# Rewriting how sums are opened and when VectorE makes its keys in a two-block transformer on one core

## The reference

```
kk = (k * k_k).reshape(b, s, h, n)
kk = kk / jnp.maximum(jnp.linalg.norm(kk, axis=-1, keepdims=True), 1e-12)
k = k * (1.0 + (a - 1.0) * k_a)
b_h = kk * a_h
def step(state, inp):
    r_t, w_t, k_t, v_t, kk_t, b_t = inp
    sa = jnp.einsum('bhvk,bhk->bhv', state, -kk_t)
    state = (state * w_t[:, :, None, :] + sa[..., None] * b_t[:, :, None, :]
             + v_t[..., None] * k_t[:, :, None, :])
    return state, jnp.einsum('bhvk,bhk->bhv', state, r_t)
_, y = lax.scan(step, state0, xs)
y = ((y - mu) * lax.rsqrt(var + RW_GN_EPS)).reshape(b, s, c) * lnx_g + lnx_b
y = (y + bonus.reshape(b, s, c)) * g
```

## Time and profile before

| what | value |
|---|---|
| median of 3 runs | 3160.74 us (3159.27 to 3164.67) |
| the profiled execution, time | 3164.66 us |
| its span in the trace | 3162.6 us |
| TensorE busy | 3033.9 us, 96% of the span |
| VectorE, ScalarE, GpSimd busy | 799.9, 469.8, 106.6 us |
| chain that ended last | TensorE 79%, SyncE's queue 10%, DMA 4%, VectorE 3% |
| mean granted TensorE clock | 0.981 |

### The profile page before, as it was taken

The page is one execution under the profiler, slowest core; times in us unless marked ns, Lnnn a source line. Parts: engine busy times, 40 slices in busy tenths (PEclk is TensorE's granted clock), DMA queues, the critical chain, the costliest instruction groups (busy, mean ns, idle before and its releaser), DMA issues.

```text
span 3162.6 us, 39204 instructions
## 1 busy us (share of the span) xinstructions
PE 3033.9 (96%) x16547; PEld 2126.2 (67%) x16547; DVE 799.9 (25%) x1677; ACT 469.8 (15%) x1074; POOL 106.6 (3%) x118
## 2 busy tenths in 40 slices
PE   7999998999999999999998999998899999999998
PEld 3566666577777777677786577786666666666665
DVE  2566666410020044300255400034000001001001
ACT  2332332000010022200121200122000000000001
POOL 1121121000000000000000000000000000000000
PEclk8999999999999999999998999998999999999999
DMA  7333117454444433254401244441999999999996
GB/s 249 115 113 127 47 55 275 152 184 151 142 145 159 133 133 100 68 158 143 154 36 41 91 158 147 151 121 37 380 384 382 384 381 382 382 383 382 380 383 255
DMA packets 403488, 636.07 MB, mean 201 GB/s; under 512 B 11247, under 2 KB 276054, under 8 KB 396030
## 3 DMA queue, kind: packets, MB, share of 16 engines
q1 hardware_dynamic: 397981, 612.29, 55.7%
q0 software_dynamic: 5344, 21.46, 1.9%
HBM read 632.51 MB, written 1.20 MB: 200 GB/s over the span
## 4 chain that ended last, share of the span: by engine, by line
PE 79%; SPq 10%; DMA 4%; DVE 3%; issue 1%; ACT 1%; DVEq 1%; PEld 0%; PEldq 0%; ACTq 0%
PE PS L925 18%; PE PS L933 7%; PE PS L1394 7%; PE PS L3835 5%; SPq L852 5%; PE PS L3862 4%; SPq L3713 3%; PE PS L3887 3%; PE PS L3850 3%; PE PS L701 2%; PE PS L1970 2%; PE PS L991 2%; PE PS L3290 2%; PE PS L1966 2%; PE PS L675 1%; PE PS L1544 1%
## 5 line engine op out<-in xcount | busy, mean ns | idle before, releaser
L925 PE MATMUL PS<-XT,WO 128*128 128x256 f32 x1344 | 296.2, 379 | 0.1
L925 PE MATMUL PS<-XT,WF 128*128 128x256 f32 x1344 | 294.6, 379 | 0.0
L925 PEld LDWEIGHTS PS<-XT,WO 128*128 128x128 f32 x1344 | 255.2, 190 | 50.5 <-issue 17.7
L925 PEld LDWEIGHTS PS<-XT,WF 128*128 128x128 f32 x1344 | 255.3, 190 | 46.2 <-issue 12.9
L1394 PE MATMUL PS<-XT,WH 128*128 128x512 f32 x512 | 241.6, 597 | 1.8 <-ACT XT L476 1.8
L952 DVE TENSOR_TENSOR scratch<-scratch,PS 128x256 f32<-128x256 f32 x70 | 29.5, 421 | 660.5 <-ACT scratch L942 660.2
L4122 DVE TENSOR_TENSOR scratch<-scratch,PS 128x128 f32<-128x128 f32 x84 | 24.2, 288 | 557.0 <-ACT scratch L4020 557.0
L3835 PEld LDWEIGHTS PS<-scratch,WO 128*128 128x128 f32 x1344 | 155.3, 192 | 12.6 <-issue 12.0
L3835 PEld LDWEIGHTS PS<-scratch,WF 128*128 128x128 f32 x1344 | 155.2, 192 | 12.4 <-issue 11.0
L3835 PE MATMUL PS<-scratch,WF 128*128 128x128 f32 x1344 | 157.0, 275 | 1.2 <-ACT scratch L3999 1.2
L3835 PE MATMUL PS<-scratch,WO 128*128 128x128 f32 x1344 | 157.0, 275 | 0.4 <-DMA WO<-in_moe_wu 0.4
(11 more groups left out here) (579 smaller groups left out, 4060.4 us busy)
## 6 DMA issues: line engine op xcount, KB each, us to landing
XT<-in_moe_wg SPq DMA_DIRECT2D x70, 1024.0 KB, 11.1
scratch<-in_moe_wu SPq DMA_DIRECT2D x70, 1024.0 KB, 13.3
WO<-in_ada_w SPq DMA_DIRECT2D x36, 1024.0 KB, 7.2
OT<-in_moe_wd SPq DMA_DIRECT2D x36, 1024.0 KB, 13.9
WF<-in_moe_wg SPq DMA_DIRECT2D x21, 1024.0 KB, 14.3
WF<-in_moe_wu SPq DMA_DIRECT2D x21, 1024.0 KB, 17.0
WF<-in_moe_wd SPq DMA_DIRECT2D x21, 1024.0 KB, 14.3
WO<-in_moe_wg SPq DMA_DIRECT2D x21, 1024.0 KB, 14.5
```

The lines of the kernel that those rows point to most:

```text
L925: mm = nc.tensor.matmul(k.PS[:, 4 + f, w * n:(w + 1) * n], slot.gu[:, w, kb, f * P:(f + 1) * P], rhs(kb), start=kb == 0, stop=kb == KB - 1)
```

## The change

There are four edits. Sums are no longer opened by `zero_sum` in the dense nets, the DeltaNet heads and the scan; their first product has `start=True` instead. `rw_tilde_vector` is split into `rw_keys_scaled_vector` (three operations) and `rw_decayed_vector` (three and the signal `til`), and for round 1 they run inside round 0's scan, behind z and behind the negated rn. "tkv" moves from place 0 to place 1 of level 2. At level 4 of round 1, `rw_out_vector` comes ahead of `mla_rope_vector`.

```diff
-def turn_tensor(k, pe, slots, order, rnds, rhs, n, hid, acc):
+def turn_tensor(k, pe, slots, order, rnds, rhs, n, hid, acc, opens=None):
...
-                                      slot.dn[:, f, half * 512:(half + 1) * 512], start=False, stop=False)
+                                      slot.dn[:, f, half * 512:(half + 1) * 512], start=(what, s, f) == opens, stop=False)
...
-    zero_sum(k, True, range(4))
-    turn_tensor(k, pe, slots, TURN[2:8], first, rhs, L, k.hid, range(4))
+    turn_tensor(k, pe, slots, TURN[2:8], first, rhs, L, k.hid, range(4), ("down", 0, 0))
...
-            zero_sum(k, True, (4,))
             project(24, 27)
...
             mm = nc.tensor.matmul(ps[:, 4, c], k.vn[:, d, :], k.att[h % 2][:, d, tile, :],
-                                  start=False, stop=t == 3 and d == 1)
+                                  start=t == 0 and d == 0, stop=t == 3 and d == 1, skip_group_check=True)
...
-    elif step == (2, 0):
+    elif step == (2, 1):
         rw_tokens_tensor(k, pe, rnd, "tkv")
-    elif step == (2, 1):
         rw_tokens_tensor(k, pe, rnd, "tk")
...
     rw_u_tensor(k, pe, rnd, 0)
-    zero_sum(k, True, (4, 5))
     for j, hh in heads:
-        nc.tensor.matmul(z(j, hh), k.tok[:, 2, 2 * j, ROWS[hh]], k.tok[:, 0, 2 * j, ROWS[hh]], start=False, stop=False)
+        nc.tensor.matmul(z(j, hh), k.tok[:, 2, 2 * j, ROWS[hh]], k.tok[:, 0, 2 * j, ROWS[hh]], start=j == 0, stop=False,
+                         skip_group_check=True)
...
-    zero_sum(k, True, (2, 3))
     for j, hh in heads:
         nc.tensor.matmul(rn(j, hh), k.gr[0][:, hh, 2 * j + 1, :], k.tok[:, 0, 2 * j + 1, ROWS[hh]],
-                         start=False, stop=False)
+                         start=j == 0, stop=False, skip_group_check=True)
...
-def rw_tilde_vector(k, dve, rnd):
+def rw_keys_scaled_vector(k, dve, rnd):
...
     tt(k.kk, k.kk, k.rtm, ALU.mult)
     dve.drain()
     tt(bt, k.kk, k.ra[:, 2 * rnd:2 * rnd + 2, :], ALU.mult)
     dve.wait_ge(*k.rwf_act.at("ws", rnd))
     tt(kap, k.kk, k.ww[:, 1, :, :], ALU.mult)
+
+
+def rw_decayed_vector(k, dve, rnd):
...
     dve.drain()
     tt(bt, bt, k.wi, ALU.mult)
     tt(rt, k.rkv[:, W_R, :, :], k.ww[:, 0, :, :], ALU.mult)
     tt(kt, kt, k.wi, ALU.mult)
     dve.drain().then_inc(*k.rwf_dve.done("til"))
...
     elif l == 4:
+        rw_out_vector(k, dve, 0)
         mla_rope_vector(k, dve, 0)
-        rw_out_vector(k, dve, 0)
...
             rw_negate_vector(k, dve, rnd, 1)
+            if rnd == 0:
+                rw_decayed_vector(k, dve, 1)
...
+            if rnd == 0:
+                rw_keys_scaled_vector(k, dve, 1)
...
     rw_scan_vector(k, dve, 0)
-    rw_tilde_vector(k, dve, 1)
     rw_bonus_vector(k, dve, 1)
```

More of the change, by code:

```diff
@@ L1606, in gdn_head_tensor @@
             if t:
-                nc.tensor.matmul(ps[:, 4, c], k.st[:, d, :], k.eg[h % 2][:, d, c], start=False, stop=False)
+                nc.tensor.matmul(ps[:, 4, c], k.st[:, d, :], k.eg[h % 2][:, d, c], start=False, stop=False,
+                                 skip_group_check=True)
             mm = nc.tensor.matmul(ps[:, 4, c], k.vn[:, d, :], k.att[h % 2][:, d, tile, :],
-                                  start=False, stop=t == 3 and d == 1)
+                                  start=t == 0 and d == 0, stop=t == 3 and d == 1, skip_group_check=True)
             if t < 3:
@@ L2488, in rw_scan_tensor @@
         mm = nc.tensor.matmul(z(j, hh), k.tok[:, 1, 2 * j, ROWS[hh]], k.ru[:, 2 * hh + j, :], start=False,
-                              stop=j == 1)
+                              stop=j == 1, skip_group_check=True)
     mm.then_inc(*S.done("z"))
-    zero_sum(k, True, (2, 3))
     for j, hh in heads:
         nc.tensor.matmul(rn(j, hh), k.gr[0][:, hh, 2 * j + 1, :], k.tok[:, 0, 2 * j + 1, ROWS[hh]],
-                         start=False, stop=False)
+                         start=j == 0, stop=False, skip_group_check=True)
     for j, hh in heads:
-        nc.tensor.matmul(y(j, hh, 0), k.ru[:, 2 * hh + j, :], k.gr[1][:, hh, 2 * j, :], start=False, stop=False)
+        nc.tensor.matmul(y(j, hh, 0), k.ru[:, 2 * hh + j, :], k.gr[1][:, hh, 2 * j, :], start=j == 0, stop=False,
+                         skip_group_check=True)
     pe.wait_ge(*V.at("z", rnd))
     for j, hh in heads:
-        mm = nc.tensor.matmul(rn(j, hh), kap[ROWS[hh], j, TCOL[1]], k.z[ROWS[hh], j, :], start=False, stop=j == 1)
+        mm = nc.tensor.matmul(rn(j, hh), kap[ROWS[hh], j, TCOL[1]], k.z[ROWS[hh], j, :], start=False, stop=j == 1,
+                              skip_group_check=True)
     mm.then_inc(*S.done("rn1"))
@@ L2503, in rw_scan_tensor @@
             nc.tensor.matmul(y(j, hh, tile), k.tok[:, 0, 2 * j + tile, ROWS[hh]], k.gr[2][:, hh, 2 * j + tile, :],
-                             start=False, stop=False)
+                             start=False, stop=False, skip_group_check=True)
     rw_u_tensor(k, pe, rnd, 1)
     for j, hh in heads:
-        nc.tensor.matmul(y(j, hh, 1), k.z[ROWS[hh], j, :], rt[ROWS[hh], j, TCOL[1]], start=False, stop=False)
+        nc.tensor.matmul(y(j, hh, 1), k.z[ROWS[hh], j, :], rt[ROWS[hh], j, TCOL[1]], start=False, stop=False,
+                         skip_group_check=True)
     if rnd == 1:
@@ L2716, in rw_query_vector @@
     i.then_inc(*k.rwf_dve.done("bo"))
-def rw_tilde_vector(k, dve, rnd):
+def rw_keys_scaled_vector(k, dve, rnd):
     tt = k.nc.vector.tensor_tensor
-    rt, kap, bt, kt = k.til[rnd]
+    _, kap, bt, _ = k.til[rnd]
     dve.wait_ge(*k.rwf_act.at("knorm", rnd))
@@ L2728, in rw_tilde_vector @@
     tt(kap, k.kk, k.ww[:, 1, :, :], ALU.mult)
+def rw_decayed_vector(k, dve, rnd):
+    tt = k.nc.vector.tensor_tensor
+    rt, _, bt, kt = k.til[rnd]
     dve.drain()
@@ L2824, in rw_first_vector @@
     rw_mix_vector(k, dve, 0, W_V)
-    rw_tilde_vector(k, dve, 0)
+    rw_keys_scaled_vector(k, dve, 0)
+    rw_decayed_vector(k, dve, 0)
     rw_bonus_vector(k, dve, 0)
```

## The result

| kernel | median of 5 runs | ratio to before |
|---|---|---|
| before | 3163.25 us (3159.27 to 3164.67) | |
| changed | 3145.91 us (3142.55 to 3147.40) | 0.9947 [0.9937, 0.9958] |

The change makes the kernel faster by about 17 us; the ratio gives 13.3 to 19.9. The profiled execution took 3145.91 us (its span in the trace is 3144.1), 18.75 less than the profiled execution of before. TensorE is busy for 3025.6 us, 8.3 less than before, so more than half of the gain is waiting time. The instruction that opened sums is left twice at the kernel's start, of 34 times.

What follows compares the result with a forecast made beforehand. TensorE's own work up to the router, with waits for VectorE, was taken as the bound. Terms 5.1 + 3.0 + 3.6 + 0.9 + 4.6 + 0.8 = 18.0 us, from the median 3160.74 to 3142.7 us; range 3138 to 3152.

Steps and rivals of the forecast that it cites:

- the rival on the clock: Half clock follows both shortened waits and the gates, so the clock gives nothing: 15.5 us gained, 3145.2 us; 20%.
- Zero products in nets and heads: Four dense nets drop four products each, 3.4 us; eight DeltaNet heads one each, 1.7 us; 5.1 taken, range 4.3 to 5.1.
- The rival that they cost nothing: Zero products only fill holes where TensorE waits anyway; only the moves count: 12.1 us gained, 3148.6 us; 9%.
- "tkv" behind g: Level 2, both rounds: g fills TensorE's wait, level 3's ax starts 1.5 us sooner each; 3.0 us, range 1.8 to 3.4.
- Keys inside the first scan: Round 1's six key operations move into the first scan, so its gates start at 1686.8 instead of 1690.39: 3.6 us.
- z comes 0.3 earlier: First scan: without its first zero pair z's mask starts 0.3 us earlier, at 1681.05 for 1681.34, limited by u's copy.
- The clock after the first scan: Round 1's gates run at 2.4 GHz without the 3.31 us wait: 0.9 us, ends 0 and 2.87.
- The output ahead of the rotary: Level 4, round 1: output fills VectorE's 4.10 us idle, masks x 3.07 us sooner; clock kept adds 1.6; sum 4.6.
- The second scan's zero pairs: Second round's scan, no keys: two zero pairs (0.86) go except what u's copy holds; 0.8 us, 0.4 at least.
- The two rivals on the weight stream: Experts' stage: stream takes the gain back, 3160.7 us, 8%; or loads fall out of step, 3168.5 us, 4%.
- 2.4 is nearer to 2.5: Round 1's wait behind the gates, about 2.4 us, was counted as dropping the clock, as one of 2.5 did elsewhere.
- One of the prediction's own signs of being wrong: Wrong if half clock follows the shortened waits, experts' stage length changes beyond 3 us, or a new wait stands at L2764.

Runs made afterwards that it cites:

- the first edit alone: Kernel before with all sums in dense nets, heads and both scans opened by their first product: 3164.75 us, ratio 1.0004 [0.9995, 1.0013].
- The fill on the kernel before: Kernel before with only the scans' openings changed, plus three idle zero products ahead of each scan: 3163.06 us, ratio 1.0000 [0.9991, 1.0009].

## Why the prediction was right, step by step

The predicted 3142.7 us is 3.2 under the measured median, inside the range. The sum of 18.0 us stands beside 17.3 (medians) and 18.75 (the two profiled executions); 2.5 of the 3.2 come from the base, since the median of before is 3163.25 over its five runs and was 3160.74 over three. The time alone doesn't tell the forecast from the rival on the clock: that one sums to 15.5, and the measured 13.3 to 19.9 takes in both. The traces do, term by term, and terms were off in both directions.

- **Zero products in nets and heads, 5.1.** Right. Alone they give 5.1 us by the medians, and the fourth net's share shows in its place: the lead grows from 19.63 us at the second scan's end (the last products at 1753.78 and 1734.15) to 20.49 there, by the 0.86 that was counted. The rival that they cost nothing falls.
- **"tkv" behind g, 2 x 1.5.** Right: 1.46 in round 0, and 1.47 in each round for the edit alone. No wait is left on the transposes.
- **Keys inside the first scan, 3.6.** From z mask to gates 3.24 less, and 0.08 at the z mask: 3.32. The order of VectorE's work came as worked out: negation 2.22 us behind the z mask (2.35 counted), decayed keys 2.73 (2.75), copy of u 4.75 (4.70), gates 5.81 (5.75). Mis-sized is the first step, "z comes 0.3 earlier". The second z products now wait 0.27 us for the copy of u, so the first zero pair had mostly been hiding behind that copy. The prediction's own figures for the copy of the second u (1685.1 and 1685.75) give a hold of 0.65 us where it says 0.5; TensorE waited 0.41. The dense queue that was weighed against the sum cost nothing extra: the decayed operations start 0.61 and 0.60 us apart (1676.17, 1676.78, 1677.38).
- **The clock after the first scan, 0.9.** Mis-sized. The mechanism for the gates is right (1.16 us instead of 2.08), but the wait of 2.40 that I counted as dropping the clock did not, so that all of the upper end came: 2.87. With the keys alone, a wait of 2.41 did drop it.
- **The output ahead of the rotary, 3.07 and 1.6 for the clock.** The move gave what it should: `ax` of level 5 starts 4.54 us earlier since level 1, which is 3.08 here and 1.46 of the second round's "tkv". The wait is 2.07, as predicted (2.1). For the clock only 0.91 came of the 1.6, since half clock followed here; with this edit alone it did not.
- **The second scan's zero pairs, 0.8.** This step failed in what it left out. 0.42 was gained in the changed kernel's second scan, the lower end, and that only as long as the clock holds. In the four profiles where it falls, the second scan takes 17.0 to 17.1 us from its first u products to the end of its last; it takes 12.9 before and 12.4 in the changed kernel. The prediction treated a zero product as time alone; the scans that have it are also those that stayed at 2.4 GHz.
- **The end.** The lead is 18.65 us at the router's counts and 18.75 at the end, so the experts' stage kept step, with the same DMA wait (8.5 for 8.6). The two rivals on the weight stream fall. Ahead of it 1.84 us went in the router's half clock, for which no term stood.

The reasoning on nearness ("2.4 is nearer to 2.5", "close to the 2.05 that left the clock up") was the weak part. Over all traces in which these waits stand unfilled and the clock is up ahead of them:

| wait | length, us | clock stayed up in | fell in |
|---|---|---|---|
| gates' masks, round 0 | 2.05 to 2.06 | 7 kernels | 5 |
| gates' masks, round 1, with the keys in the scan | 2.40 to 2.41 | 3 | 2 |
| x at level 5, round 1, with the output first | 2.07 to 2.08 | 2 | 3 |

The first of these waits in two kernels, with only the nets' and heads' openings changed (clock up) and the whole change with the scans' zero products (clock fell):

```profile
1620.30 0.71 PE L2436 MATMUL PS<-mats,WO 128*128 128x128 f32 x4 [2.06 <-DVE WO L2873]
...
1623.69 1.22 PE L2435 MATMUL PS<-mats,WO 128*128 128x128 f32 x4 [2.05 <-DVE WO L2872]
```

So length doesn't decide here. The Trainium skill's "TensorE: Matmul & The Clock Gate", Part 1, calls the activity window free-running; both outcomes at one length agree with that, but the kernels differ and no run here shows the window itself. Chance is not the only reading: in round 0 the clock fell in five of the six kernels that have no zero products in the nets and heads, and in none of the six that have them. What ran long before may therefore matter, and no run tests it.

One of the prediction's own signs of being wrong came true: half clock followed a shortened wait, at level 5. The errors on the clock happened to offset each other in part: 2.0 more than counted behind the first scan, 0.7 less at level 5, 1.6 lost in round 0 and 1.8 in the router, and the luck of about 2.8 between the nets. That is luck, and not working.

Open is why the first edit alone lost the clock in both scans, while the changed kernel's profile kept it in both with the same scan. Its place in time differs, but no run here moved only that. That half clock inside a scan goes with the lack of wide zero products in or ahead of it is what the count over the profiles says; what about them keeps the clock isn't shown. The fill on the kernel before gave back less than that would, and what else its longer runs lost isn't known.

## What to carry to other kernels

Take each edit's stretch from the trace and add the gains; of a wait that an edit removes, only what is not late next is gained, and worked out so two of the moved pieces came true within 0.1 us ("tkv" 1.46 of 1.5, the output 3.08 of 3.07). A product that computes nothing may still earn its time: before removing wide products from a stretch of small ones, look at the granted clock there, and try the same products in TensorE's waits. Here they delayed nothing: with eight of them in the wait of 2.40 us, 0.68 of it was left, and the products behind it started at the same 1683.36. And measure the parts of an edit that repeats at several places apart: here one half gave 5 us and the other took it back.

## What was not expected of the hardware

- TensorE fell to 1.2 GHz inside five scans, each behind a stop of 0.83 to 0.88 us and with no stop over 1.12 us in the ten microseconds ahead of it. The rows after the fall show it busy for 6.00 of 6.00 us and 10.20 of 10.20. In the 12 scans with two pairs of 128x512 zero products, behind the same last stops, it did not.
- Waits of equal length (2.05 to 2.06 us in round 0, 2.07 at level 5) were followed by half clock in some kernels and by full clock in others, so their length alone gives no price.
